# First attention of a two-block transformer kernel: in each step of TensorE, the value products of two macros ago are put ahead of the turns (transposes) of one macro ago

## The reference, cut to what matters

```
s = einsum("bhqd,bhkd->bhqk", q[block], k[:e]) * scale
s = s + log_f_cum[q] - log_f_cum[k]
p = softmax(where(mask, s, -inf))
out[block] = einsum("bhqk,bhkd->bhqd", p, v[:e])
```

## Time and profile before

| | |
|---|---|
| median of 3 runs | 1708.41 us (1708.31 to 1710.09) |
| the profiled execution's own time | 1710.62 us |
| its span, first to last instruction | 1708.8 us |
| TensorE busy in the span | 98% |
| mean granted TensorE clock | 0.994 of full |
| first attention in the trace | about 858.6 to 952 us |

### The profile page before, as it was taken

The page is one execution under the profiler, slowest core; times in us unless marked ns, Lnnn a source line. Parts: engine busy times, 40 slices in busy tenths (PEclk is TensorE's granted clock), DMA queues, the critical chain, the costliest instruction groups (busy, mean ns, idle before and its releaser), DMA issues.

```text
span 1708.8 us, 23543 instructions
## 1 busy us (share of the span) xinstructions
PE 1681.0 (98%) x9382; PEld 1405.3 (82%) x9382; DVE 587.9 (34%) x1176; ACT 653.0 (38%) x988; POOL 688.8 (40%) x538
## 2 busy tenths in 40 slices
PE   6999999999999999999999999999999999999999
PEld 6787889898888888887866898888888887887887
DVE  3359325440100001521146240100011545788661
ACT  4653534442222222522356342222222535554651
POOL 3533233434444455544322434444455433554002
PEclk9999899999999999999999999999999999999999
DMA  5212110422222322232220122222322232222001
GB/s 197 74 54 95 51 50 26 160 75 99 98 98 98 110 99 98 72 126 99 75 75 2 52 73 99 98 98 98 127 99 98 92 106 99 75 78 95 26 2 49
DMA packets 23427, 145.00 MB, mean 85 GB/s; under 512 B 3504, under 2 KB 4272, under 8 KB 7344
## 3 DMA queue, kind: packets, MB, share of 16 engines
q1 hardware_dynamic: 23344, 143.83, 24.0%
HBM read 141.72 MB, written 2.10 MB: 84 GB/s over the span
## 4 chain that ended last, share of the span: by engine, by line
PE 68%; issue 14%; POOL 10%; DVE 5%; ACT 2%; DMA 1%; SPq 0%; POOLq 0%; ACTq 0%; DVEq 0%
POOL wlo L2804 10%; PE PS L452 5%; PE PS L453 5%; PE PS L454 5%; PE PS L485 4%; PE PS L343 4%; PE PS L346 4%; PE PS L338 4%; PE PS L486 4%; PE PS L487 4%; PE PS L961 2%; PE PS L466 2%; PE PS L467 2%; PE PS L468 2%; PE PS L1642 2%
## 5 line engine op out<-in xcount | busy, mean ns | idle before, releaser
L2804 POOL TENSOR_TENSOR wlo<-wraw,whi 128x512 fp32r<-128x512 f32 (+1 forms) x476 | 628.3, 1352 | 907.2 <-ACT whi L145 907.2
L145 ACT ACTIVATE whi<-wraw 128x2048 fp32r<-128x2048 f32 (+1 forms) x119 | 225.7, 1896 | 239.9 <-PE PS L346 183.6
L452 PE MATMUL PS<-hT_hi,whi 128*128 128x512 f32 x704 | 274.0, 389 | 0.0
L453 PE MATMUL PS<-hT_lo,whi 128*128 128x512 f32 x704 | 273.9, 389 | 0.0
L454 PE MATMUL PS<-hT_hi,wlo 128*128 128x512 f32 x704 | 273.9, 389 | 0.0
L1544 DVE TENSOR_TENSOR act_sb<-sil,PS 128x512 f32 x44 | 30.3, 688 | 428.5 <-ACT sil L1519 428.5
L1519 ACT ACTIVATE sil<-PS 128x512 f32<-128x512 f32 x44 | 26.4, 599 | 355.3 <-PE PS L454 335.4
L452 PEld LDWEIGHTS PS<-hT_hi,whi 128*128 128x128 f32 x704 | 132.2, 188 | 28.0 <-issue 0.6
L454 PEld LDWEIGHTS PS<-hT_hi,wlo 128*128 128x128 f32 x704 | 132.2, 188 | 27.5
L453 PEld LDWEIGHTS PS<-hT_lo,whi 128*128 128x128 f32 x704 | 132.2, 188 | 27.2
L485 PE MATMUL PS<-whi,hT_hi 128*128 128x512 f32 (+2 forms) x288 | 112.3, 390 | 0.1
(11 more groups left out here) (410 smaller groups left out, 3057.8 us busy)
## 6 DMA issues: line engine op xcount, KB each, us to landing
wraw<-wpack SPq DMA_DIRECT2D x125, 1024.0 KB, 4.9
gain<-gains SPq DMA_DIRECT2D x10, 512.0 KB, 6.6
x_sb<-x SPq DMA_DIRECT2D x8, 512.0 KB, 6.4
out<-x_sb SPq DMA_DIRECT2D x3, 512.0 KB, 2.6
csb<-consts SPq DMA_DIRECT2D x1, 704.0 KB, 13.7
out<-x_sb SPq DMA_DIRECT2D x2, 256.0 KB, 2.0
vh<-vecs SPq DMA_DIRECT2D x1, 96.0 KB, 6.4
small<-vecs SPq DMA_DIRECT2D x1, 80.0 KB, 12.1
```

The source lines that it names most:

```text
L145: act.activation((whi[q % 2] if static is not None else hi_of_slot(n))[:, w], wraw[q % 2][:, w], ACT.Copy).then_inc(w_hi, 1)
L452: nc.tensor.matmul(o, whi[q][w], hT_hi[:, k, :], start=(k == 0), stop=False)
L453: nc.tensor.matmul(o, whi[q][w], hT_lo[:, k, :], start=False, stop=False)
L2804: p.tensor_tensor(lo[:, a:b], wraw[q][:, a:b], hi[:, a:b].bitcast(F32), ALU.subtract).then_inc(w_lo, 1)
```

## The change

In each step, `pe_values(m - 2)` is issued after the scores and the hook, ahead of `pe_sums` and `pe_turn(m - 1)`; before, it came after both. Nothing else differs: every instruction, wait, buffer and count is the same, and the orders of ScalarE, VectorE, POOL and SP are not touched.

```diff
                     if m in hooks:
                         hooks[m]()
+                    if 0 <= m - 2 < self.n:
+                        self.pe_values(m - 2)
                     if m % 4 == 1 and m > 4:
                         self.pe_sums(m // 4 - 1)
                     if 0 <= m - 1 < self.n:
                         self.pe_turn(m - 1)
-                    if 0 <= m - 2 < self.n:
-                        self.pe_values(m - 2)
```

## The result

The kernel after takes 1711.3 us (median of 18 runs), the kernel before 1708.3 us beside it: the ratio is 1.0022, with a 95% interval of 1.0013 to 1.0031, that is 2.2 to 5.3 us slower. By the two medians the difference is 3.0 us, by the ratio 3.8; two runs of the kernel before, of 2503 and 3388 us, are left out of the ratio. The forecast was 3.7 us slower and 1712.1 us, with 1710.0 to 1715.5 as the range.

What follows compares the result with a forecast made beforehand. TensorE bounds the stretch, with 9.54 us of work and 0.32 of waiting per 9.86 us period. Seven steps C at 0.16 plus seven steps D at 0.37 give 3.7 us; added to 1708.4 that is 1712.1 us, range 1710.0 to 1715.5.

Steps and rivals of the forecast that it cites:

- What bounds the stretch: Attention's four-step period of 9.86 us: TensorE is the bound, with 9.54 us of work and 0.32 of waiting.
- Step A: Scores of block 3, values of block 2, sums, turn of block 0: cost 0, ending at 2.90 us, before 2.93.
- Step B: Scores of block 1, values of block 0, turn of block 3: ends at 5.35 us as before, cost and gain 0.
- Step C: Scores of block 2, values of block 3, turn of block 1: new 0.16 us wait for ScalarE's copy.
- Step D: Scores of block 0, values of block 1, turn of block 2: new 0.37 us wait for VectorE's copy.
- Scores to values: New TensorE pass between pieces, unseen in the trace; taken as hidden where TensorE waits, like other passes; sum stays 3.7 us.
- Neither bound: Limits for scores to values: -1.4 us if free in 8 steps A, +3.6 us if added behind 21 waits.
- The start and the end: First step C and last step D hide their copies, first step D costs 0.37: seven steps C and seven steps D.
- that sign: First tile of "fo", behind the attention: would start near 947.3 instead of 943.56.
- the turns did not wait for their exponentials: Rival: turns waited for exponentials, values fill all 3.5 us of TensorE's waits, giving 1704.9 us; chance 0.04.
- rival 1: Step B's wait goes because ScalarE's copy of block 0 slips ahead: 2.0 us back, sum +1.7, 1710.1 us; chance 0.08.
- The clock did not fall once a pair: Rival: granted clock falls to half once a pair, 7 x 1.6 = 11 us on top, 1723 us; chance 0.04.

Runs made afterwards that it cites:

- e7: Kernel before, old order, with VectorE copying blocks 0, 1 and 2 and both engines copying one head each of block 3: 1702.3 us, ratio 0.9972.
- e8: Copies of e7 plus the values ahead in steps D and A: 1702.6 us in one execution; timed again 1703.2 us, ratio 0.9978.
- e1: Kernel before with the values ahead only in steps D and A, old order in B and C: 1707.0 us, ratio 0.9999.
- e6: Kernel before, old order, with the copy of block 0 moved from ScalarE to VectorE: 1704.6 us, ratio 0.9978.
- e2: Kernel before with the values ahead only in step B: 1706.4 us in one execution.
- e4: Kernel after with every copy split by head, ScalarE and VectorE copying one head each at once: ratio 1.0006.
- e3: Kernel before with the values ahead only in step C: 1707.5 us in one execution.
- e9: Kernel after with VectorE copying only the first head of block 1 from the second pair on, output not valid: period 10.13 us, one execution.

## Why the prediction was right

- **What bounds the stretch.** TensorE with 9.54 us of work and 0.32 of waiting: shown by e7 and e8, whose periods of 9.58 and 9.55 us are what is left when the copies are out of the way.
- **Step A, cost 0.** Measured 2.90 us, as written out; e1 has the new order in D and A and no loss. The 0.03 us is not gained there, since the wait of step B ends when it did.
- **Step B, nothing either way.** Its wait is of the same size and now stands ahead of the values. e6 shows its cause: with the copy of block 0 out of ScalarE's queue it is gone.
- **Step C, 0.16.** Measured 0.17, and e2 gives 0.17 for the order of step B alone. In e4, with the copy halved, step C is back at 2.63 us.
- **Step D, 0.37.** Measured 0.37, and e3 gives 0.37 for the order of step C alone. e9 shortens the copy by 0.27 us and the step by 0.27.
- **Scores to values.** The one pass that no row showed was taken as the others. In step A after, the values start at 897.01, 1.29 after the scores; the estimate had the same 1.29. Neither bound came true: the pass is not free, and behind a wait it adds nothing (902.19 to 902.25, 904.66 to 904.71). The Trainium skill's rule (TensorEngine Tiling (Array Packing), Key Properties), that a change of tiling mode drains the engine, agrees with the trace here. With a change of shape the next load comes 0.59 us after the start of four transposes (903.27 to 903.86), without one 0.39 us (944.82 to 945.21, below). Two readings of the prediction were off without harm. Not every pass shows 0.17 us of idle weight load: before the turn at 904.60 there is no such bracket; what the passes share is that the next load begins 0.07 us ahead of the modelled end. And there are seven steps A with values in them, not eight, so the lower bound was -1.2 us.
- **The start and the end.** This is where the account was loose, and where it had some luck. The first step C was held to be free, since it ran at half clock before. In the profile after the clock did not fall, so it cost its 0.16 (2.79 us against 2.63), and the stretch was spared the 1.56 us of slow clock. With the stretch also beginning 0.39 us sooner in its span, that is why the profiled span grew by only 1.6 us, from 1708.8 to 1710.4, and the first tile came at 945.21 and not near 947.3: that sign missed. Against e1, where the clock did not fall either, the new order costs 79.43 - 75.79 = 3.64 us. The steps add up to that but for 0.02: seven steps D at 0.37 and eight steps C at 0.17 are 3.95, less 0.08 in the first step B (4.10 against 4.18) and 0.21 at the end, where the last step C takes 2.59 instead of 2.80, since the turn and the first tile of "fo" have the same shape and follow each other without a pass. So the forecast of 3.7 left out 0.17 in the first step C and 0.29 the other way, and the two largely cancel. The rows of the last step C:

```profile
944.82 0.42 PEld L1799 LDWEIGHTS PS<-csb,fp 128*128 128x128 f32 x4 [0.17 <-issue]
...
945.21 0.30 PEld L338 LDWEIGHTS PS<-whi,hT_hi 128*128 128x128 f32 x2
```

- **Behind the attention** nothing was given back, as said: 756.8 us before, 756.9 after.

The rivals: the turns did not wait for their exponentials, since not one wait for L1845 has gone or come ahead of a turn. Step B's wait did not go, as rival 1 had it (0.23 us of TensorE's own in step B after, 0.22 before). The clock did not fall once a pair: outside the start it was 1.00 through the stretch. If the kernel before lost its 1.6 us of clock in every execution and the kernel after in none, the difference would be 79.43 - 77.39 = 2.0 us, just below the interval of 2.2 to 5.3; how often the timed executions lose it, no run shows.

## What to carry to other kernels

On an in-order engine that hands work to another and takes it back, ask of each hand-over what lies between it and the first instruction that waits for its return. Work put *ahead* of the producing piece is no cover for it; put behind, it is. Write out one period with the starts from the trace, for every block size, since a reordering that is free beside the long piece costs beside the short one, and then look whose queue the remaining wait is: here moving one copy to the other engine and splitting another was worth about 0.3%. The order alone cost 0.2% in all four steps, nothing that the times show in D and A, and with the copies out of the way it gained 0.2 us there in the trace (e8 against e7).

## What the runs showed of the hardware

- At a change of shape between scores, values and turns, in every direction that the runs have, the next load begins some 0.07 us before the modelled end of the last matmul. Behind turns and values that leaves the weight load idle for 0.17 us. Behind four transposes the change costs 0.20 us (0.59 against 0.39 from their start to the next load). When a wait for another engine ends later than that, the change adds nothing.
- After a wait of 2.0 us on TensorE (2.27 for the weight load) the granted clock went from 1.00 to 0.50 for some 3 us in two profiles and stayed at 1.00 in two others with the same instructions up to there, a difference of 1.6 us.
- VectorE instructions that wait for nothing started some 0.08 us before the row of the one ahead ended (e8: 0.34 and 0.60 us from start to start where the rows are 0.42 and 0.68 long), so that summing their lengths overstated the queue.
